# Linear attention: the topmost score level as a product of 64 weight columns and 64 moving columns

## What is computed

```
S_t = diag(a_t) S_{t-1} + k_t^T v_t;   o_t = q_t S_t
scores[i, j] = sum_k q[i, k] k[j, k] exp(cum[i, k] - cum[j, k])      for j <= i within a chunk
o_intra = scores @ v
```

## Time and profile before

| what | value |
|---|---|
| device time, median of 3 runs | 2165.16 us (2161.14 to 2166.86) |
| the profiled execution: span from its first to its last instruction | 2163.2 us |
| PE busy | 2091.5 us, 97% of the span |
| DVE busy | 1259.9 us, 58% |
| POOL busy | 938.3 us, 43% |
| ACT busy | 765.7 us, 35% |

### The profile page before, as it was taken

The page is one execution under the profiler, slowest core; times in us unless marked ns, Lnnn a source line. Parts: engine busy times, 40 slices in busy tenths (PEclk is TensorE's granted clock), DMA queues, the critical chain, the costliest instruction groups (busy, mean ns, idle before and its releaser), DMA issues. The chain is left out here.

```text
span 2163.2 us, 30139 instructions
## 1 busy us (share of the span) xinstructions
PE 2091.5 (97%) x10120; PEld 1708.6 (79%) x10120; DVE 1259.9 (58%) x1857; ACT 765.7 (35%) x1336; POOL 938.3 (43%) x825
## 2 busy tenths in 40 slices
PE   6999999999999999999998999997999999999999
PEld 4788888887777877877776788885888888888887
DVE  5658686852468568568567564558444444444444
ACT  3333343311346446446446300016323333222232
POOL 3423232323434434434435233447655555565552
PEclk8999999999999999999999899998999999999999
DMA  4112121222431431431543722220211111111112
GB/s 125 43 30 58 30 57 24 60 69 73 98 89 38 107 92 34 108 94 32 107 95 112 263 78 73 88 68 20 79 58 58 58 58 39 58 43 35 58 58 78
DMA packets 137777, 153.86 MB, mean 71 GB/s; under 512 B 7664, under 2 KB 112112, under 8 KB 137728
## 3 DMA queue, kind: packets, MB, share of 16 engines
q1 hardware_dynamic: 136000, 150.07, 25.4%
q10 hardware_dynamic: 1728, 3.15, 0.4%
HBM read 107.06 MB, written 20.97 MB: 59 GB/s over the span
## 5 line engine op out<-in xcount | busy, mean ns | idle before, releaser
L123 POOL TENSOR_TENSOR w_hi<-w_raw,w_ones 128x64 fp32r<-128x64 f32 x88 | 35.9, 408 | 677.0 <-PE gla_g L149 307.3
L525 POOL TENSOR_TENSOR sb_rows<-sb_beta,sb_rest 128x128 f32<-128x128 f32 (+7 forms) x128 | 154.3, 1206 | 227.0 <-DVE sb_rest L912 199.7
L127 POOL TENSOR_TENSOR w_lo<-w_raw,w_hi 128x512 fp32r<-128x512 f32 x176 | 241.2, 1391 | 7.3
L912 DVE TENSOR_TENSOR_SCAN sb_rest<-sb_rest 128x128 f32<-128x128 f32 (+7 forms) x128 | 209.9, 1640 | 39.2 <-ACT sb_beta L756 39.2
L918 DVE TENSOR_TENSOR sb_wt_lo<-sb_t,sb_wt_hi 128x512 fp32r<-128x512 f32 (+2 forms) x186 | 103.2, 555 | 124.5 <-ACT sb_wt_hi L764 122.4
L149 PE MATMUL sb_g<-h_hi,w_hi 128*128 128x512 f32 x544 | 156.3, 414 | 2.7 <-DVEq L815 1.9
L149 PE MATMUL sb_g<-h_hi,w_lo 128*128 128x512 f32 x544 | 151.9, 404 | 0.0
L149 PE MATMUL sb_g<-h_lo,w_hi 128*128 128x512 f32 x544 | 151.2, 402 | 0.0
L764 ACT CAST sb_wt_hi<-sb_t 128x512 fp32r<-128x512 f32 (+2 forms) x186 | 89.6, 482 | 167.2 <-PE sb_t L627 166.0
L149 PE MATMUL gla_g<-h_hi,w_hi 128*128 128x512 f32 x480 | 129.9, 406 | 3.5 <-DVEq L1377 3.5
L2024 POOL TENSOR_TENSOR ff_w_lo<-raw_g,ff_w_hi 128x512 fp32r<-128x512 f32 x66 | 85.6, 1296 | 109.7 <-ACT ff_w_hi L2140 109.7
(11 more groups left out here) (378 smaller groups left out, 5076.0 us busy)
## 6 DMA issues: line engine op xcount, KB each, us to landing
w_raw<-w_in SPq DMA_DIRECT2D x64, 512.0 KB, 8.1
raw_g<-w_ffn_gate SPq DMA_DIRECT2D x11, 1024.0 KB, 5.5
ff_raw_u<-w_ffn_up SPq DMA_DIRECT2D x11, 1024.0 KB, 5.8
ff_raw_d<-w_ffn_down SPq DMA_DIRECT2D x11, 1024.0 KB, 4.8
sb_qs<-sb_q_st SPq DMA_DIRECT2D x32, 256.0 KB, 5.1
sb_kh<-sb_k_st SPq DMA_DIRECT2D x32, 256.0 KB, 5.0
sb_kl<-sb_k_st SPq DMA_DIRECT2D x32, 256.0 KB, 5.0
mp_sig<-gates_t SPq DMA_DIRECT2D x16, 512.0 KB, 4.3
```

The costliest lines, as they stand in the source:

```text
L123: self.nc.gpsimd.tensor_tensor(hi[:, 0:64], raw[:, 0:64], self.ones[:], ALU.mult)
L127: ins = self.nc.gpsimd.tensor_tensor(lo[:, at], raw[:, at], hi[:, at], ALU.subtract)
L525: nc.gpsimd.tensor_tensor(rows[tb // 4][:, tb % 4, 0:width], beta[:, n % 2, 0:width], rest[:, n % 2, 1:width + 1], ALU.mult).then_inc(row_ ...
L912: nc.vector.tensor_tensor_scan(back, back, back, 1.0, ALU.mult, ALU.bypass).then_inc(scanned, 1)
```

## The change

Level 6 is taken out of the loop over the levels. Its product takes the first 64 tokens of the chunk as weights and the last 64 as moving columns, and writes 64 partitions and 64 columns of `SC`, those that the mask keeps. The other three quarters of `SC[:, 6, :]` are no longer written by it; the masks multiply what stands there by zero. Levels 0 to 5 and the diagonal are as before. It runs once for each chunk, 32 times.

```diff
@@ -1181,8 +1181,12 @@
                     pe.wait_ge(t_free, t_uses(it) + ch)
                     nc.tensor.transpose(T[:, 0:P], k_out[:, at], c["ident"][:]).then_inc(t_done, 1)
                     pe.wait_ge(s_free, s_uses(it) + ch + 1)
-                    for lv in range(LEVELS - 1):
+                    for lv in range(LEVELS - 2):
                         nc.tensor.matmul(SC[:, lv, :], X[:, lv, at], X[:, lv, at], start=True, stop=True)
+
+                    mid = ch * P + P // 2
+                    nc.tensor.matmul(SC[0:P // 2, LEVELS - 2, P // 2:P], X[:, LEVELS - 2, ch * P:mid],
+                                     X[:, LEVELS - 2, mid:(ch + 1) * P], start=True, stop=True)
                     nc.tensor.matmul(SC[:, LEVELS - 1, :], k_diag[:, at], q_diag[:, at],
                                      start=True, stop=True).then_inc(s_done, 1)
```

## The result

| | before | changed |
|---|---|---|
| device time, median of 5 runs | 2163.03 us (2161.14 to 2166.86) | 2172.0 us (2170.22 to 2173.61) |
| span of the profiled execution | 2163.2 us | 2171.5 us |
| PE busy | 2091.5 us | 2098.5 us |

The ratio of the runs is 1.0039, with a 95% interval of 1.0027 to 1.005: the change makes the kernel slower by some 9 us (5.8 to 10.8). Two single runs of the experiments, 2608.81 us with 65 columns and 4223.84 us with 64 weight and 128 moving columns, lie far from all others and are left out of the ratios; they move the medians shown by 0.2 and 0.3 us. The prediction, 2163.4 us and no change that can be told, was wrong, and its range ended at 2168.0.

What follows compares the result with a forecast made beforehand. TensorE (PE) was taken as the bound; 57 ns saved per chunk over 32 chunks gave 1.8 us, so span 2163.2 became 2161.4, plus 2.0 for the median: 2163.4 us, range 2158.5 to 2168.0.

Steps and rivals of the forecast that it cites:

- A step: Time from one TensorE load or MATMUL to the next in the scores, 0.112 us before; each product has two.
- not two: Rival that both steps of level 6 halve: 115 ns a chunk, 3.7 us in all, 2161.5 us; chance 7%.
- the rule: Each score step is the longer of 0.83 ns per moving column and 0.875 ns per weight column of the next load.
- the inner step: Between the two halves of level 6's product: from 112 to 57 ns, 55 gained.
- 107 there: Step from level 5's last half to level 6's first: 128 columns still stream, 112 to 107 ns, 5 gained.
- the stop: Rival: array empties at both switches around the narrow product, 326 ns a chunk, 8.6 us slower, 2173.8 us; chance 5%.
- both switches: Changes from 128 to 64 array columns and back around a narrow product, claimed to occur without a gap before the change.
- rows 8: Profile rows around L640 and L643, cited against the stop: loads 0.12 and 0.06 us apart around a 64-column product.
- the open part: Admitted doubt: the products cited against the stop aren't of the plain 32-bit kind on both sides.
- My price of 163 ns a stop: Cost of each switch around the narrow product if the array must empty: 275 - 112 = 163 ns.

Runs made afterwards that it cites:

- the trimmed levels: Kernel before, but each level takes only weight and moving columns its mask keeps, never under 65 weight columns: 2157.71 against 2163.61 us, ratio 0.997.

## Why the prediction was wrong

- **PE bounds, and a change to its stream goes through one to one.** Right: 230 ns in each chunk reached DVE's waits as 7.5 us and the end as 9 (5.8 to 10.8); PE's waits stayed within 0.4 us, and so did, on balance, the stretch behind 475 us.
- **A step is the longer of the moving columns and the next load; 64 columns save one step of 55 ns, not two.** Right as a mechanism, where no gap opens: 65 columns gave 55 ns of the 57, 64 moving columns alone nothing, and the trimmed levels 171 ns of the 186 that the rule gave. In the changed kernel only the inner step is as forecast: the second narrow load starts at 127.939 us and its MATMUL at 127.992, 53 ns for 57. The 55 ns between the two narrow loads are no sign of it, since the forecast had 107 there.
- **The step that failed is the dismissal of the stop, at 5%.** I wrote that "both switches stand in rows 8". They didn't: the products there are rounded, and rounded ones are the exception. I saw it as "the open part" and yet gave it no weight. Two stops were priced at 326 ns, less 57 of gain 269; measured were 285 less 55, that is 230. A gap costs about 0.10 us beyond the streaming, and the load that follows it lies open. My price of 163 ns a stop, the recorded length of a MATMUL less one step, isn't made of these two parts; that it came near is partly luck.
- **The row that would have decided was in the trace of before.** L1153, at six places in this stretch, is unrounded, fills 16 of 128 rows and stands between full products; at all six its first load begins 0.31 us behind the last one. I looked at the products that resembled the change in the number of columns and not in the type.
- **A rule that I had at hand named the loss, and I went by rows that didn't bear on it.** The Trainium skill, page "TensorEngine Tiling (Array Packing)", section "Key Properties", says that a change of the tiling mode drains the TensorE. The trace doesn't record a mode. If 64 weight columns or 16 rows mean another mode than 128, it agrees for unrounded 32-bit and bf16 products, with about 0.10 us a switch beyond the streaming columns and a load that isn't hidden, and doesn't agree for rounded ones.

What stays open: why rounded products of 64 columns stand among full ones without a gap, and what the 0.10 us consist of. Rounded ones may run on the whole array whatever their width; no run here tells.

## What to carry to other kernels

An unrounded product of 64 weight columns, or of 16 rows, among full ones is no small product: it brings a gap ahead of it and one behind, here some 285 ns against 55 saved. Take 65 columns, put narrow ones one right behind the other, or fill up the rows. Other widths below 64 and other counts of rows weren't run for this type. When a row of the trace is to clear a doubt, it must be like the change in every property that could matter, the type included; and a halved product is worth only the step of which both the streaming and the next load are shorter.

## What the runs showed that I had not expected

- 64 and 65 weight columns differ by 285 ns per chunk (2.242 against 1.957 us), the wider one being the faster.
- Rounding the operand takes away both gaps; bf16 doesn't (114 ns less, 342 more per chunk).
- The loads of the trimmed levels follow the column count without steps from 127 down to 65: 189, 190, 188, 184, 178, 164 and 138 ns each for 127, 126, 124, 120, 112, 96 and 65 columns, and starts at uneven columns took no visible toll (171 ns saved per chunk of 186 summed).
